# Layer 1's modulation: seven chunks multiplied on VectorE, TensorE summing the partitions

## The reference, cut to what matters

```
mod   = silu(c)     @ w_mod[l] + b_mod[l]      # 6 x 1024 values
mod_c = silu(c_ctx) @ w_mod[l] + b_mod[l]
sh1, sc1, g1, sh2, sc2, g2 = split(mod, 6)
h = rms_norm(x) * (1 + sc1) + sh1              # and the same for the context
u = h @ w_in[l]                                # columns of four head groups
x = x + g1 * (concat(attention groups) @ w_out[l])
h2 = rms_norm(x) * (1 + sc2) + sh2
x = x + g2 * moe(h2)
```

## Time and profile before

| | us |
|---|---|
| median of 3 runs | 1576.59 |
| lowest and highest | 1574.71, 1581.21 |
| the profiled execution | 1579.66 |
| its span, first to last instruction | 1577.8 |
| mean granted TensorE clock in it | 0.995 |
| PE, DVE, ACT, POOL busy | 1533.6, 823.4, 417.2, 190.7 |

### The profile page before, as it was taken

The page is one execution under the profiler, slowest core; times in us unless marked ns, Lnnn a source line. Parts: engine busy times, 40 slices in busy tenths (PEclk is TensorE's granted clock), DMA queues, the critical chain, the costliest instruction groups (busy, mean ns, idle before and its releaser), DMA issues.

```text
span 1577.8 us, 26136 instructions
## 1 busy us (share of the span) xinstructions
PE 1533.6 (97%) x9918; PEld 1035.2 (66%) x9918; DVE 823.4 (52%) x1796; ACT 417.2 (26%) x922; POOL 190.7 (12%) x356
## 2 busy tenths in 40 slices
PE   6999999999999999999999999999999999999996
PEld 4655446766665577788888655556666667788883
DVE  2323524467676676454545721524567766644446
ACT  1322113355554410100000412113455541000001
POOL 0111110000000000212121110210000000122212
PEclk9999999999999999999999999999999999999998
DMA  9642111731001487689898771113711035688884
GB/s 360 200 146 107 54 50 65 227 135 41 15 28 41 140 320 275 221 316 343 328 335 295 285 258 54 54 53 117 243 63 41 15 108 189 229 301 309 318 321 186
DMA packets 103210, 283.50 MB, mean 180 GB/s; under 512 B 18728, under 2 KB 32552, under 8 KB 93352
## 3 DMA queue, kind: packets, MB, share of 16 engines
q1 hardware_dynamic: 91728, 261.03, 46.5%
q0 software_dynamic: 10800, 20.99, 3.5%
q10 hardware_dynamic: 584, 0.14, 0.0%
HBM read 262.52 MB, written 38.53 MB: 191 GB/s over the span
## 4 chain that ended last, share of the span: by engine, by line
PE 90%; DVE 4%; DMA 2%; issue 2%; ACT 1%; POOL 1%; SPq 0%; DVEq 0%; POOLq 0%; ACTq 0%
PE S L1300 18%; PE S L1693 16%; PE B L1466 8%; PE S L1386 8%; PE S L1704 8%; PE PT L1407 5%; PE B L1443 5%; PE B L1321 3%; PE B L1204 3%; PE PT L1618 2%; DMA arena<-in_w_mod 2%; PE S L1321 2%; PE S L1557 1%; PE S L1577 1%; PE PT L1577 1%
## 5 line engine op out<-in xcount | busy, mean ns | idle before, releaser
L1300 PE MATMUL S<-arena 128*128 128x512 f32 (+3 forms) x768 | 296.0, 535 | 2.4 <-ACT arena L962 2.4
L1693 PEld LDWEIGHTS S<-arena 128*128 128x128 f32 x2304 | 263.0, 192 | 17.2 <-issue 17.2
L1693 PE MATMUL S<-arena 128*128 128x128 f32 x2304 | 263.5, 275 | 0.0
L1300 PEld LDWEIGHTS S<-arena 128*128 128x128 f32 x768 | 139.9, 190 | 122.6 <-issue 102.3
L1069 ACT ACTIVATE arena<-S,nmax 128x768 f32<-128x768 f32 (+1 forms) x200 | 154.8, 778 | 144.9 <-DVE nmax L2190 120.7
L2190 DVE TENSOR_REDUCE nmax<-S 128x1 f32<-128x768 f32 (+1 forms) x168 | 133.2, 826 | 70.6 <-PE S L1386 60.5
L1466 PE MATMUL B<-arena 128*128 128x512 f32 x320 | 153.7, 602 | 0.6 <-DVE arena L2248 0.5
L1386 PE MATMUL S<-arena 64*128 64x256 f32 (+5 forms) x624 | 135.2, 472 | 2.2 <-ACT arena L1069 2.2
L1407 PEld LDWEIGHTS PT<-cst,arena 128*128 128x128 f32 x768 | 86.9, 141 | 65.3 <-issue 51.9
L1704 PE MATMUL S<-arena 128*128 128x512 f32 x288 | 129.5, 592 | 0.0
L1407 PE MATMUL PT<-cst,arena 128*128 128x128 f32 x768 | 114.5, 278 | 5.2 <-issue 4.0
(11 more groups left out here) (325 smaller groups left out, 1752.6 us busy)
## 6 DMA issues: line engine op xcount, KB each, us to landing
arena<-in_w_mod SPq DMA_DIRECT2D x24, 2048.0 KB, 10.7
arena<-in_moe_w_gate SPq DMA_DIRECT2D x36, 1024.0 KB, 7.3
arena<-in_moe_w_up SPq DMA_DIRECT2D x36, 1024.0 KB, 9.0
arena<-in_moe_w_down SPq DMA_DIRECT2D x36, 1024.0 KB, 5.2
arena<-in_w_in SPq DMA_DIRECT2D x6, 2048.0 KB, 8.0
arena<-y SPq DMA_DIRECT2D x20, 512.0 KB, 5.9
arena<-mod SPq DMA_DIRECT2D x16, 512.0 KB, 7.0
arena<-in_tokens SPq DMA_DIRECT2D x12, 512.0 KB, 9.8
```

The costliest lines, as they stand in the source:

```text
L1300: mm = pe.matmul(ubank[u % 4][:, c0:PANEL_W[p]], hT[:, k, t * P:(t + 1) * P], panel[p][:, k, c0:], start=k == 0, stop=k == KT - 1)
L1693: mm = pe.matmul(to, wgu[b][:, w, k * DE + h * P:k * DE + (h + 1) * P], XT[b][:, k, :], start=k == 0, stop=k == KT - 1)
```

## The change

In layer 1, chunks 4 to 10 are no longer multiplied by TensorE. DVE forms, for each of the 8 `k`, the weight row times the per-partition value of silu(c) and adds it to an accumulator [128, 512] (`mod_part`): one `tensor_scalar` for k = 0 and seven `scalar_tensor_tensor`, each waiting for the one before. TensorE sums the 128 partitions with four matmuls against a matrix of ones (`mod_sum`), into the bank that `mod_row` reads. All 56 `mod_part` calls stand at the end of DVE's loop turns u = 0 to 15 (three each) and 18 to 20 (three, three, two), in the order of chunks; `mod_sum` stands in units 4, 7, 9, 12, 15, 17 and 22. Chunk 11 stays a `mod_product` and takes the place of chunk 7 at the opening of attention; nothing of the modulation is left in the attention steps. The loads move with it, on SP, and are freed by `mod_acc`, DVE's count of finished chunks. Only the latent stream's modulation is made for these chunks. One semaphore, `x1_sq`, is folded into `small_exp` to make room. Layer 0 is as before.

```diff
-MODS_LATE = {u + 2: n for u, n in MODS_AT.items()}
+V_MODS = range(4, 11)
+V_MOD_AT = {u: [] for u in range(NTU)}
+for _i in range(KT * len(V_MODS)):
+    V_MOD_AT[_i // 3 if _i < 48 else 18 + (_i - 48) // 3].append((V_MODS[_i // KT], _i % KT))
+MODS_LATE = {4: 4, 7: 5, 9: 6, 12: 7, 15: 8, 17: 9, 22: 10}
+AT_OPENING = (FAR, NMCH - 1)
+FAR_AT = (FAR_STEPS, {})
...
-                 mod_late + [slot[1], mod_w5, slot[2], mod_w5] + [slot[2]] * 2 + [mod_w2, slot[2], mod_w2]]
+                 mod_late + [slot[1], mod_w5, slot[2], mod_w5, slot[2], mod_w5] + [slot[2]] * 3]
...
                     mod_load(1, 5, 0)
+                    mod_load(1, 6, 0, 1)
                     win_load(1, 2, T)
-                    for n in range(6, 8):
-                        mod_load(1, n, n - 1)
+                    mod_load(1, 7, 0, 2)
+                    mod_load(1, 8, 0, 3)
+                    mod_load(1, 9, 0, 4)
                     win_load(1, 3, 2 * T)
+                    mod_load(1, 10, 0, 6)
                     win_load(1, 4, 3 * T)
+                    mod_load(1, 11, 0, 7)
                     mod_store(1)
...
+                def mod_sum(n, bank):
+
+                    pe.wait_ge(s["mod_acc"], n - V_MODS[0] + 1)
+                    for q in range(4):
+                        mm = pe.matmul(bank[32 * q:32 * q + 32, 0:MODQ], ones[:, 0:32], mod_acc[n][:, q * MODQ:(q + 1) * MODQ], start=True, stop=True)
                     mm.then_inc(s["mod_mm"], 1)
...
                             pe.wait_ge(s["mod_row"], NMCH * l + mod)
-                            mod_product(l, mod, B6)
+                            if l:
+                                mod_sum(mod, B6)
+                            else:
+                                mod_product(l, mod, B6)
...
-                pe.wait_ge(s["mod_row"], NMCH * l + FAR)
-                mod_product(l, FAR, B6)
+                pe.wait_ge(s["mod_row"], NMCH * l + AT_OPENING[l])
+                mod_product(l, AT_OPENING[l], B6)
...
-                    if n in FAR_STEPS:
+                    if n in FAR_AT[l]:
...
+                def mod_part(n, k):
+
+                    acc, w = mod_acc[n], mod_w[1][n][:, k, :]
+                    if k == 0:
+                        which, count = mod_in(1, n)
+                        dve.wait_ge(s[f"mod_w_in{which}"], count)
+                        if n == V_MODS[-1]:
+                            dve.wait_ge(s["hT_tr"], 2 * T)
+                        elif n - V_MODS[0] >= 2:
+                            dve.wait_ge(s["mod_mm"], NMCH + n - 1)
+                        ins = dve.tensor_scalar(acc, w, cs[:, k, 0:1], None, ALU.mult)
+                    else:
+                        ins = dve.scalar_tensor_tensor(acc, w, cs[:, k, 0:1], acc, ALU.mult, ALU.add)
+                    if k == KT - 1:
+                        ins.then_inc(s["mod_acc"], 1)
+                    else:
+                        prep_ch.done(ins).sync()
...
                     if 0 <= u - 19 < T:
                         diff_apply(u - 19)
+                    if l:
+                        for n, k in V_MOD_AT.get(u, []):
+                            mod_part(n, k)
```

More of the change, by code:

```diff
@@ L318, in program @@
         assert take.at[0] <= QKV_END + 6 * 352 + 3 * 384 + 2 * 768 + 2 * 384
+        take = region(WIN_END + (SL_DK + 1) * NTOK)
+        acc_0, acc_1 = take(MCH), take(MCH)
+        assert take.at[0] <= WIN_END + (SL_DQ + 2) * NTOK
+        acc_last = arena[:, XT_START + 2 * D - 832:XT_START + 2 * D - 832 + MCH]
+        mod_acc = {n: (acc_0, acc_1)[n % 2] for n in V_MODS[:-1]}
+        mod_acc[V_MODS[-1]] = acc_last
         take = region(0)
@@ L471, in program @@
                  "xa_in", "scored", "neg_max", "exp_done", "rinv_ready", "comb_done", "p_tr", "pt_v", "pt_s", "pv_done", "o_v", "o_s",
-                 "v_o", "d_stat", "d_rs", "rinv_wide", "d_fin", "op_mm", "res_mul", "x1_ready", "x1_sq",
+                 "v_o", "d_stat", "d_rs", "rinv_wide", "d_fin", "op_mm", "res_mul", "x1_ready", "mod_acc",
                  "h2_scaled", "h2_ready", "x1_stored", "h2_stored", "s_g2_in",
@@ L625, in mod_rows, with mod_load @@
                             sp.dma_start(mod_norm_at(l, half)[r:P:32], gain.rearrange("(n q c) -> q n c", q=4, c=MODQ)).then_inc(s["mod_rows_in"], 16)
-                def mod_load(l, n, free):
+                def mod_load(l, n, free, taken=0):
+                    if taken:
+                        sp.wait_ge(s["mod_acc"], taken)
                     if free:
@@ L744, in _ @@
                         sp.dma_start(qk[96:P, to, SEQ:NTOK], qk[rows, SL_DK + i // 2, SEQ:NTOK]).then_inc(copies_in, 16)
-                mod_load(l, 8, 8)
                 if l == 0:
+                    mod_load(0, 8, 8)
                     mod_load(0, 9, 9)
@@ L757, in _ @@
                 sp.dma_start(wout[:, 2:4, :], A["w_out"][l][2 * P:4 * P, :].rearrange("(k p) n -> p k n", p=P)).then_inc(s["wout_in"], 16)
-                mod_load(l, 11, 10)
-                sp.wait_ge(s["mod_mm"], NMCH * (l + 1) - l)
+                if l == 0:
+                    mod_load(0, 11, 10)
+                sp.wait_ge(s["mod_mm"], NMCH * (l + 1))
                 sp.dma_start(wout[:, 4:KT, :], A["w_out"][l][4 * P:D, :].rearrange("(k p) n -> p k n", p=P)).then_inc(wout_late_in, 16)
@@ L1100, in x1_square @@
                     act.wait_ge(s["x1_ready"], g(t) + 1)
-                    act.activation(h2b, xb, ACT.Square, scale=D ** -0.5, accum_out=h2s[:, 0:1]).then_inc(s["x1_sq"], 1)
+                    act.activation(h2b, xb, ACT.Square, scale=D ** -0.5, accum_out=h2s[:, 0:1]).then_inc(s["small_exp"], 1)
                 nt = tiles_of(l)
@@ L1205, in mod_product @@
                                            start=k == 0, stop=k == KT - 1)
+                    mm.then_inc(s["mod_mm"], 1)
+                def mod_sum(n, bank):
+                    pe.wait_ge(s["mod_acc"], n - V_MODS[0] + 1)
+                    for q in range(4):
+                        mm = pe.matmul(bank[32 * q:32 * q + 32, 0:MODQ], ones[:, 0:32], mod_acc[n][:, q * MODQ:(q + 1) * MODQ], start=True, stop=True)
                     mm.then_inc(s["mod_mm"], 1)
@@ L1850, in x1_rstd @@
                 def x1_rstd(t):
-                    pool.wait_ge(s["x1_sq"], g(t) + 1)
+                    pool.wait_ge(s["small_exp"], g(t) + 3 + l)
                     pool.tensor_tensor(h2s[:, 1:2], h2s[:, 0:1], eps8[:, 0:1], ALU.add).then_inc(s["g_x"], 1)
@@ L2155, in _ @@
                 ch.done(dve.tensor_scalar(subg[:, :], subg[:, :], 1.0 - lam_init, None, ALU.mult))
-                dve.wait_ge(s["small_exp"], l + 2)
+                dve.wait_ge(s["small_exp"], 2 + (T + 1) * l)
                 ch.done(dve.tensor_tensor(nlam[:, 2:3], nlam[:, 1:2], nlam[:, 0:1], ALU.subtract)).sync()
@@ L2265, in h2_shift @@
                     dve.tensor_tensor(h2b, h2b, vec[:, 2 if t < TL else 5, :], ALU.add).then_inc(s["h2_ready"], 1)
-                mod_row(l, FAR, B6[:, :])
+                mod_row(l, AT_OPENING[l], B6[:, :])
+                if l:
+                    mod_gain(1, 1)
                 if l == 0:
```

2 lines of the change are left out of this document (removed).

## The result

| | before | after |
|---|---|---|
| median of 16 runs each, us | 1577.41 | 1584.11 |
| lowest and highest | 1574.71, 1581.21 | 1581.20, 1587.43 |
| the profiled execution | 1579.66 | 1582.20 |
| its span | 1577.8 | 1580.4 |
| mean granted clock in it | 0.995 | 0.993 |

What follows compares the result with a forecast made beforehand. TensorE, 97% busy, was taken as the bound. Projection +10.3 us and attention -7.7 us sum to +2.6: 1582.3 us against the profiled 1579.66, or a median of 1579.2, in a range of 1571 to 1588.

Steps and rivals of the forecast that it cites:

- First wait: Unit 4 of layer 1's projection: TensorE waits 9.2 us for DVE's chunk 4, queued behind an evacuation and spare_pairs.
- DVE's chunk: DVE's work for one chunk: eight dependent steps, 6.0 us, with 0.78 us taken for a step.
- lor_ready: Unit 7's lor round: held by chunk 5's load and DVE's queue, at 936.0 in place of 924.69, 11.3 us late.
- chunk 6 late: Rival, chance 0.16: chunk 6's load lands at 936.8, lor_ready 3.9 us later; with the step 7 gap staying, 1586.9 us.
- The clock: PE's clock falls to the 1.2 GHz level after idling; the loss behind the second wait, before unit 7's round, costs 1.6 us.
- Sums: TensorE's seven sums in layer 1's projection, 0.24 us each, in place of products of 1.88 us.
- DVE's other due times hold: Rest of layer 1's projection: DVE's three added steps, 2.4 us a unit, come after urgent work and delay nothing.
- The sum of the projection: Layer 1's projection in all: 11.3 + 1.6 - 3.76 + 1.2 = +10.3 us.
- Attention: First tile: -7.7 us; step 4 gains 1.35, step 6 nothing, step 9 0.65, step 7 5.7 with its gap gone.
- the gap stays: Rival, chance 0.30: step 7's idle gap remains, attention gains only 3.9 us, +6.4 us in all, 1583.0.
- The median: The whole kernel's median: 1579.2 us, +2.6 over the kernel before.

Runs made afterwards that it cites:

- x1: The changed kernel with only the sum of chunk 4 moved from unit 4 to unit 6: 1587.54 us, ratio 1.0065 to the kernel before.
- x10: The changed kernel with 20 unused filler matmuls of 256 columns ahead of the first sum in unit 4: 1584.08 us, ratio 1.0046 to the kernel before.
- x4: The changed kernel with DVE's mod_row of each layer-1 chunk one turn later: 1582.06 us, ratio 1.0019 to the kernel before.
- x9: The kernel before with one of eight k of chunk 9's product in attention step 6, layer 1: 1577.95 us, ratio 0.9996.
- x8: The kernel before with one of eight k of the products of chunks 8 to 11 in layer 1, loads kept: 1572.48 us, ratio 0.9960.
- x0: The changed kernel run and profiled once more, unedited: 1584.25 us, ratio 1.0043 to the kernel before.
- x5: The changed kernel with chunk 4's sum in unit 7, chunks 5 to 9 behind lor_apply(0), and mod_row one turn later: 1570.99 us, ratio 0.9945 to the kernel before.

## Why the prediction was right, step by step

The mechanisms held in the main, the two waits and what attention gives back. The size of the sum owes something to luck, as terms that were too large and terms that were missing came out nearly even; and one mechanism, the cause of the gap in step 7, was wrong though its number came true.

- **First wait** (forecast 9.2, measured 8.99): right in cause and size. The hidden `spare_pairs` loop, taken as 1.7 us, was 1.44. That this wait alone decides nothing was predicted and is shown by x1.
- **DVE's chunk** (6.0): 0.48 + 5.47 us and a hand-over, 6.0 in all, a step 0.75 us, as worked out from the widths 768 and 1024.
- **`lor_ready`** (+11.3 with 1.6 of clock behind it): the round came 9.90 us late. Chunk 5's load landed 9.06 us after its issue, not 9.8, and DVE's chain took 9.3 us, not 9.9. This is the mis-sized term, 3.0 us with the next. The rival "chunk 6 late" did not occur: its load landed 13.7 us after its issue, not 19.2, and DVE took its first step at 930.82 without waiting.
- **The clock** (1.6 exposed behind the second wait): the mechanism is right, its place wrong. The loss was 2.3 us, stood behind the first wait, and used up the second, so that the clock never fell a second time. x10 shows that it cost nothing. I had let the first wait's loss disappear in the second, rightly, but expected 2.3 to 3.9 us of wait to be left before the round, and only 0.26 were: this loss was set too small (1.6) and DVE's side too late. The Trainium skill, page "TensorE: Matmul & The Clock Gate", section "Part 1: The HAM clock gate", has the low clock as the default that activity must release; the trace agrees, with 0.50 for five microseconds of busy PE after the 8.99 us of wait. Behind the 2.0 us of step 6 one profile shows 0.50 and another 1.00.
- **Sums** (0.24 each): 0.35 to 0.36 from their start to the next instruction. Over the five sums behind the round that is +0.6 us. The form's price was taken from a product of 64 records; that a group's start costs something which the 64 share is a guess that no run tests.
- **"DVE's other due times hold"**: wrong, +1.9 us. I had counted steps and loads and not the row: `mod_row`, moved with its chunk to another turn, waits for a sum in the middle of its unit at the head of DVE's queue. x4 removes the two waits. The sum of the projection, 9.90 - 3.76 + 1.8 + 1.93 = 9.9 and 0.7 more unassigned, is 10.54 beside a forecast of 10.3. This is luck: 3.0 us too much in the round and its clock hid 3.2 us too little behind it.
- **Attention** (-7.7, measured -7.10): from the values of the step to the next transposes, step 4 gained 1.3 us (forecast 1.35) and step 9 0.65 (0.65), and from step 7's values to its transposes 5.9 us went (5.7). Some 0.8 us of this was lost to short waits that the prediction did not have, 0.42 of them for ACT before the scores of step 8. Step 6 gives nothing (x9; the releaser is ACT's last exponential, which ends 0.1 us after the copy I had named), and the gap of step 7 goes (x8), but not for the reason given. The loads were named as its cause; x8 leaves them in place and loses the gap. The rival "the gap stays" (0.30) turned on this cause, and I had it wrong: with the four products kept and only the loads moved, I would now expect the gap to stay, which no run tests.
- **The median.** By stages, without the landmark, the profiled execution of after is 3.7 us over before, the second one (x0) 5.9; the medians say 6.7. In 8 of its 16 runs the changed kernel took at most 1583.0, at mean clocks of 0.992 to 0.994, and in 8 at least 1585.2, at 0.989 to 0.992. A low clock behind the new wait of step 6 can be one part of this, up to 2.4 us (x0); the landmark's own movement, up to 3.1 us, can be another. The spread does not come from the first wait's low clock alone: with that wait filled, in x10, four runs took 1582.8 to 1584.1 us at 0.996 and 0.997, and three 1586.3 to 1588.0 at 0.992 to 0.994. How much each has of the 6.7 stays open. The profiled execution of before lay 2.2 us over its median of 16, that of after 1.9 under.

## What to carry over

Moving work from a busy engine to one that is idle on average pays only where it stands behind the idle engine's urgent work and its result is asked for late enough; here both had to move, since each alone left a wait of 9 us, at the same sum or one later. Where a row, a load or a result moves with the work, walk the whole in-order queue at its new place, not only the added instructions. A product that fills a wait costs nothing, so taking it away gains nothing (step 6). By the traces the gain of the best version, x5, is 2.6 us in the projection and 7.1 us in attention, where the gap went.

## What the hardware showed that was not expected

GpSimd's small operations took longer beside the steps of a chunk on DVE. Three `TENSOR_TENSOR` of six values a partition took 0.20, 0.20 and 1.32 us in before, and beside three steps of a chunk, in the changed kernel:

```profile
1010.83 2.32 DVE L2059 SCALAR_TENSOR_TENSOR arena<-arena,cs 128x512 f32<-128x512 f32 x3
1010.99 0.64 POOL L1848 TENSOR_TENSOR gqa_m<-gqa_s,halfs 128x6 f32<-128x6 f32 x1 [10.46 <-DVE gqa_s L2132]
1011.71 0.71 POOL L1849 TENSOR_TENSOR gqa_m<-gqa_m,halfs 128x6 f32<-128x6 f32 x1
...
1012.49 1.83 POOL L1850 TENSOR_TENSOR gqa_r<-gqa_m,halfs 128x6 f32<-128x6 f32 x1
...
1014.36 0.56 DVE L2143 TENSOR_TENSOR arena<-arena,gqa_r 128x384 f32<-128x384 f32 x1 [1.21 <-POOL gqa_r L1850]
```

DVE then waits 1.21 us for the result, in the chain that ends in PE's wait for the `gqa` round; no run tests how much of the 1.9 us above hangs on it. At 1018.68 us in the same trace, where DVE runs no step, the three again took 0.20, 0.20 and 1.32. And a filler of 256 columns in float32 costs two records of some 0.22 us (20 took 8.82 us), so that a wait is best filled by counting records from a trace.
